# The recurrence's output gate moved from GpSimd (tokens on partitions) to VectorE (features on partitions)

## The reference, cut to what matters

```python
proj = jnp.einsum('bsd,de->bse', rms_norm(x, attn_norm_g), w_in)
qd, kd, vd, qr, fr, ir, gr = jnp.split(proj, SPLIT_POINTS, axis=-1)
od = differential attention of qd, kd, vd, normalised by head
orr = hgrn2_chunked(silu(qr), 1 - f, ir, log f)        # gated linear recurrence
orr = rms_norm(orr, hgrn_norm_g) * jax.nn.silu(gr)      # the gate of this case
mix = jnp.concatenate([od, orr], axis=-1)
x = x + mix @ w_out;  x = x + SwiGLU(rms_norm(x))
```

## Time and profile before

| what | value |
|---|---|
| median of three runs | 2685.63 us (2679.19 to 2687.0) |
| profiled execution | 2681.91 us, span 2680.2 us |
| TensorE busy | 2565.4 us, 96% |
| VectorE busy | 1574.3 us, 59% |
| ScalarE busy | 1143.0 us, 43% |
| GpSimd busy | 900.8 us, 34% |
| granted TensorE clock, mean | 0.985 |

### The profile page before, as it was taken

The page is one execution under the profiler, slowest core; times in us unless marked ns, Lnnn a source line. Parts: engine busy times, 40 slices in busy tenths (PEclk is TensorE's granted clock), DMA queues, the critical chain, the costliest instruction groups (busy, mean ns, idle before and its releaser), DMA issues. The chain is left out here.

```text
span 2680.2 us, 39239 instructions
## 1 busy us (share of the span) xinstructions
PE 2565.4 (96%) x15720; PEld 2150.4 (80%) x15720; DVE 1574.3 (59%) x1927; ACT 1143.0 (43%) x1917; POOL 900.8 (34%) x601
## 2 busy tenths in 40 slices
PE   7999999999898989888999999999999999999999
PEld 6888888887787878786877888887888887888887
DVE  5424344332777777776567666667666666456653
ACT  4434334332467777775563222224232223322221
POOL 4001100000515151404446554554555452236300
PEclk9999999999899999998999999999999999999999
DMA  4755565474544444317784333336334335777763
GB/s 158 266 173 191 196 209 186 137 255 131 136 103 116 107 116 107 86 53 241 235 292 144 103 112 92 106 103 196 106 104 116 93 100 186 260 263 276 240 202 130
DMA packets 343909, 430.79 MB, mean 161 GB/s; under 512 B 19248, under 2 KB 212784, under 8 KB 341040
## 3 DMA queue, kind: packets, MB, share of 16 engines
q1 hardware_dynamic: 343728, 428.29, 50.7%
HBM read 301.87 MB, written 129.50 MB: 161 GB/s over the span
## 5 line engine op out<-in xcount | busy, mean ns | idle before, releaser
L629 DVE TENSOR_TENSOR proj_w_lo<-proj_w_raw,proj_w_hi 128x2048 fp32r<-128x2048 f32 x56 | 130.1, 2323 | 230.1 <-ACT proj_w_hi L529 230.1
L791 PE MATMUL proj_prod<-proj_w_hi,proj_h_lo 128*128 128x512 f32 x640 | 250.1, 391 | 0.0
L1897 ACT ACTIVATE feed_a_hi<-lend_shared 128x1024 fp32r<-128x1024 f32 (+1 forms) x78 | 93.8, 1202 | 286.7 <-PE feed_v_bank L2201 142.0
L1195 ACT ACTIVATE att_expo<-att_ring,att_neg_max 128x1024 f32<-128x1024 f32 (+4 forms) x192 | 164.9, 862 | 101.8 <-DVE att_neg_max L1316 65.7
L2199 PE MATMUL feed_y_bank<-feed_b_hi,feed_a_hi 128*128 128x512 f32 x416 | 165.7, 398 | 16.4 <-DVE feed_results L2054 10.3
L1897 ACT ACTIVATE feed_a_hi<-ahead_full 128x1024 fp32r<-128x1024 f32 (+1 forms) x78 | 93.4, 1202 | 186.1 <-PE feed_y_bank L2201 136.9
L2018 DVE TENSOR_TENSOR feed_a_lo<-lend_shared,feed_a_hi 128x1024 fp32r<-128x1024 f32 (+1 forms) x78 | 148.5, 1904 | 26.8 <-ACT feed_a_hi L1897 26.8
L2201 PE MATMUL feed_y_bank<-feed_b_hi,feed_a_lo 128*128 128x512 f32 x416 | 163.8, 394 | 0.0
L2199 PE MATMUL feed_v_bank<-feed_b_hi,feed_a_hi 128*128 128x512 f32 x416 | 162.9, 392 | 0.4 <-DVE feed_results L2072 0.4
L2201 PE MATMUL feed_v_bank<-feed_b_hi,feed_a_lo 128*128 128x512 f32 x416 | 162.0, 389 | 0.0
L2200 PE MATMUL feed_v_bank<-feed_b_lo,feed_a_hi 128*128 128x512 f32 x416 | 161.9, 389 | 0.0
(11 more groups left out here) (337 smaller groups left out, 7335.4 us busy)
## 6 DMA issues: line engine op xcount, KB each, us to landing
proj_w_raw<-in_w_in_dram SPq DMA_DIRECT2D x56, 1024.0 KB, 6.5
lend_shared<-in_w_gate_dram SPq DMA_DIRECT2D x88, 256.0 KB, 4.0
ahead_full<-in_w_up_dram SPq DMA_DIRECT2D x88, 256.0 KB, 4.0
ff<-ahead_results SPq DMA_DIRECT2D x88, 256.0 KB, 2.5
ff<-ahead_ff_sum SPq DMA_DIRECT2D x66, 256.0 KB, 3.2
operands<-ahead_results SPq DMA_DIRECT2D x48, 256.0 KB, 3.2
lend_lent<-ff SPq DMA_DIRECT2D x28, 384.0 KB, 3.3
down_f_raw<-ff SPq DMA_DIRECT2D x28, 384.0 KB, 3.3
```

Of the source, the lines that this page charges most:

```text
L629: nc.vector.tensor_tensor(w_lo[n % 2][:], w_raw[n % 2][:], w_hi[n % 2][:].bitcast(F32), ALU.subtract).then_inc(w_lo_made, 1)
L791: last = pe.matmul(prod[t][:], lo[:, s, tile], wh[:, k, :], start=False, stop=stop)
L1195: nc.scalar.activation(expo[b][:, m, key:key + width], ring[:, bank * 512:bank * 512 + width], ACT.Exp, bias=neg_max[:, b, m:m + 1], accum ...
L1897: nc.scalar.activation(a_hi[:, first:end], full[g % 2][:, first:end], ACT.Copy).then_inc(a_hi_made, 1)
```

## The change

The gate stays in feature form from the projection on. `project` computes the group HG with the weights stationary, as HQ and HF, and `hgate` has the shape (W, SEQ). In `mix_tokens` the GpSimd product L1154 and the semaphore `r_gated` are gone. Chunks 4 to 7 are no longer copied by ScalarE: VectorE reads the transposed chunk from PSUM, multiplies by the column of gains and by the gate's rows, and writes the stage buffer, one step after the chunk was transposed, ahead of `maximum(s, 0)`. It signals `chunk_gated`, which takes the place of `slot_taken` and of `staged` for these chunks. SyncE loads the gate of block h once the four chunks of head h - 1 are gated (from step 11 of head h on) and ahead of the next block's k, instead of at step 6. The order of head 3's chunks becomes 0, 4, 5, 1, 6, 2, 7, 3, and their taking is shared between the engines.

```diff
-                    HI: lambda: [tokens("hv")], HG: lambda: [tokens("hgate")]}[kind(gi)]()
+                    HI: lambda: [tokens("hv")], HG: lambda: [features("hgate")]}[kind(gi)]()
-                        if kind(gi) in (HQ, HF):
+                        if kind(gi) in (HQ, HF, HG):
-    LAST_CHUNKS = (0, *range(TURNS, CHUNKS), *range(1, TURNS))
+    LAST_CHUNKS = (0, TURNS, *(c for n in range(1, TURNS) for c in (TURNS + n, n)))
+    GATED, TAKEN = [key[0] == "f" and key[2] >= TURNS for key in SLOT], []
+    for n, gates in enumerate(GATED):
+        TAKEN.append(GATED[:n + 1].count(gates))
+        rgate = r.sb("gate", [P, HEADS, TB])
+        def wait_taken(eng, slot):
+            eng.wait_ge(chunk_gated if GATED[slot] else slot_taken, TAKEN[slot])
             def store(h, c):
-                sp.wait_ge(staged, n + 1)
+                if c < TURNS:
+                    sp.wait_ge(staged, h * TURNS + c + 1)
+                else:
+                    sp.wait_ge(chunk_gated, h * HEADS + c - TURNS + 1)
-                    sp.wait_ge(r_gated, h)
-                    load_tokens(rgate, "hgate", h, rgate_in)
+                sp.wait_ge(chunk_gated, h * HEADS)
+                load_features(sp, mid["hgate"], h, rgate[:], rgate_in)
-                nc.gpsimd.tensor_tensor(ro[:], ro[:], rgate[:], ALU.mult).then_inc(r_gated, 1)
-                    act.wait_ge(r_gated, h + 1)
+                    act.wait_ge(fill_read, filled(h, len(FILLS) - 1))
                 for head, c in chunks_at(s):
-                    take_chunk(head, c)
+                    if c < TURNS:
+                        take_chunk(head, c)
+            def gate_chunk(h, c):
+                slot, n = SLOT["f", h, c], chunk_number(h, c)
+                dve.wait_ge(slot_turned, slot + 1)
+                dve.wait_ge(rgate_in, 16 * (h + 1))
+                if h == HEADS - 1:
+                    dve.wait_ge(slot_turned, SLOT["w", TOTAL - 2, groups_of(TOTAL - 2) - 1] + 1)
+                elif n >= STAGES:
+                    dve.wait_ge(stored[n % STAGES], 16 * (n // STAGES))
+                nc.vector.scalar_tensor_tensor(out=staged_at(h, c), in0=turned[slot % 2][:], scalar=rg_col[:],
+                                               in1=rgate[:, c - TURNS, :], op0=ALU.mult, op1=ALU.mult).then_inc(chunk_gated, 1)
                 if early:
                     combine(s - 1)
+                for head, c in chunks_at(s - 1) if s < TOTAL else ():
+                    if c >= TURNS:
+                        gate_chunk(head, c)
                 if live:
                     maximum(s, 0)
...
                     nc.vector.tensor_tensor(first_b[0], first_b[0].bitcast(F32), first_hi.bitcast(F32), ALU.subtract)
+                    gate_chunk(HEADS - 1, TURNS)
                 if s == TOTAL + 1:
+                    gate_chunk(HEADS - 1, TURNS + 1)
                     invert_last_roots()
                     normalise_late(LATE_CHUNKS[-1])
+                    for c in range(TURNS + 2, CHUNKS):
+                        gate_chunk(HEADS - 1, c)
```

More of the change, by code:

```diff
@@ L957, in mix_tokens @@
         rq, rk, rf = early.rows(0), early.rows(1), early.rf
-        rv, rgate = (r.sb(n, [P, CH, W]) for n in ("v", "gate"))
+        rv = r.sb("v", [P, CH, W])
+        rgate = r.sb("gate", [P, HEADS, TB])
         whole = [None] + [r.sb(f"whole{m}", [P, HEADS * TB >> m]) for m in range(1, LEVELS + 1)]
@@ L1008, in mix_tokens @@
         r_summed = r.sem("summed")
-        r_gated = r.sem("gated")
+        chunk_gated = r.sem("chunk_gated")
         r_rms_made = r.sem("rms_made")
@@ L1101, in _ @@
                     load_tokens(rv, "hv", 0, rv_in)
-                    load_tokens(rgate, "hgate", 0, rgate_in)
                 if not last:
@@ L1147, in behind_combination @@
                     pool.wait_ge(combined, step)
-            def gate(h):
-                pool.wait_ge(rgate_in, 16 * (h + 1))
-                pool.wait_ge(fill_read, filled(h, len(FILLS) - 1))
-                if h + 1 < HEADS:
-                    pool.wait_ge(combined, (h + 1) * STEPS - 1)
-                nc.gpsimd.tensor_tensor(ro[:], ro[:], rgate[:], ALU.mult).then_inc(r_gated, 1)
             nc.gpsimd.memset(rscore[:], 0.0).then_inc(scores_cleared, 1)
@@ L1187, in _ @@
                     product(h + 1, LEVELS - 1)
-                gate(h)
         @block.scalar
@@ L1212, in take_chunk @@
                     act.wait_ge(stored[n % STAGES], 16 * (n // STAGES))
-                col = g_col if c < TURNS else rg_col
-                nc.scalar.activation(staged_at(h, c), turned[slot % 2][:], ACT.Copy, scale=col[:]).then_inc(slot_taken, 1)
-                act.wait_ge(slot_taken, slot + 1)
+                nc.scalar.activation(staged_at(h, c), turned[slot % 2][:], ACT.Copy, scale=g_col[:]).then_inc(slot_taken, 1)
+                wait_taken(act, slot)
                 act.sem_inc(staged, 1)
@@ L1388, in normalise_late @@
                     dve.wait_ge(r_rrms_made, HEADS)
-                    dve.wait_ge(r_gated, HEADS)
+                    dve.wait_ge(fill_read, filled(h, len(FILLS) - 1))
                     head = c - TURNS
@@ L1470, in open_slot @@
                 if slot >= 2:
-                    pe.wait_ge(slot_taken, slot - 1)
+                    wait_taken(pe, slot - 2)
             def turn(s, g):
@@ L1484, in weigh @@
                 h, j = divmod(s, STEPS)
-                pe.wait_ge(slot_taken, SLOT["w", s, g] + 1)
+                wait_taken(pe, SLOT["w", s, g])
                 if g == 0 and s:
@@ L2515, in hybrid_trunk_kernel @@
         "hq": scratch("hq", (W, SEQ)), "hf": scratch("hf", (W, SEQ)), "hk": scratch("hk", (W, SEQ)),
-        "hv": scratch("hv", (SEQ, W)), "hgate": scratch("hgate", (SEQ, W)),
+        "hv": scratch("hv", (SEQ, W)), "hgate": scratch("hgate", (W, SEQ)),
     }
```

## The result

| kernel | median of 12 runs | lowest to highest | profiled execution | its span | mean granted clock |
|---|---|---|---|---|---|
| before | 2685.59 us | 2679.19 to 2693.46 | 2681.91 us | 2680.2 us | 0.985 |
| after | 2696.59 us | 2691.18 to 2702.38 | 2697.78 us | 2696.1 us | 0.980 |

The ratio after to before is 1.0041, with an interval from 1.0030 to 1.0051. The forecast was 2685 us with a range up to 2694; the change costs 11 us, and the sum had it at +1.3. Most of what the change does came as the working had it. One term (the product of step 8, +2.3 us) was too small by a factor of three, and another (the end of the stage, -1.0 us) had the wrong sign.

What follows compares the result with a forecast made beforehand. TensorE, busy 96%, was taken as the bound, its gaps in `mix_tokens` hanging on a chain headed by VectorE. Terms 0 + 0 + 0 + 0 + 2.3 - 1.0 = +1.3 us gave 2683.2 or 2686.9; forecast 2685 us, range 2676 to 2694.

Steps and rivals of the forecast that it cites:

- The product of step 8: `mix_tokens`, three heads: VectorE's new product delays maximum, exponentials and TensorE's next score by its length, +2.3 us.
- the end of the stage: End of `mix_tokens`: last chunk taken 1.9 us sooner, so last `mix` stores and `feed` come sooner, -1.0 us.
- Projection: `project`: four gate groups move to feature form with matmul number and size unchanged, cost 0.
- GpSimd's product: `mix_tokens`: four GpSimd products of 4.54 us go, none on the path, worth 0.
- ScalarE's copies: `mix_tokens`, heads 1 to 3: twelve copies go, 10.1 us of ScalarE's time, taken as worth 0.
- The rival that ScalarE was the limit: `mix_tokens`: the saved 0.84 us in twelve places reach TensorE, -8.8 us in all, 2675 us; chance 0.12.
- The products of steps 9 to 11: `mix_tokens`, nine places: products of 0.75 us fit VectorE's gaps of about 0.96 us ahead of the maxima, cost 0.
- the slower rival: `mix_tokens`: GpSimd's reads hold up the new products or they don't fit, +10.2 us, 2694 us; chance 0.14.
- The rule that was weighed there: VectorE with two SBUF inputs blocks against GpSimd reading SBUF; with at most one, like the new product, it doesn't.
- The upper bound of 6.7 us: Step 8's product in three heads: cost of 3 x (0.75 + 1.49) us if GpSimd holds it up.
- The waits added: `mix_tokens`: VectorE's wait for a stored stage buffer and the later gate load, 0 for both.
- ScalarE's wait for the stores: `feed`: sign that the forecast is right, ScalarE's wait for `mix` falls from 2.39 us to below 1 us.

Runs made afterwards that it cites:

- e5_no_pool: Kernel before, with GpSimd's product of the gate done on one column instead of all: 2686.53 us, ratio 0.9996.
- e2_behind_max: Changed kernel with VectorE's product in step 8 put behind the first maximum instead of ahead of it: 2688.66 us, ratio 1.0002.
- e14_behind_old_order: Changed kernel with step 8's product behind the first maximum and the last head's chunks in the order of the kernel before: 2688.33 us, ratio 1.0006.
- e11_one_step_later: Changed kernel with the chunks of heads 0 to 2 turned one step later (FIRST_CHUNK_STEP 4 in place of 3): 2689.85 us, ratio 1.0009.
- e12_later_old_order: Changed kernel with FIRST_CHUNK_STEP 4 in place of 3 and the last head's chunks in the old order: 2686.68 us, ratio 1.0004.
- e7_extra_gaps: Kernel before, with an added VectorE reduction of 512 columns in steps 9, 10 and 11 of heads 1 to 3: 2685.04 us, ratio 0.9999.
- e3_one_column: Changed kernel with its twelve VectorE products of heads 0 to 2 working on one column of 512: 2689.87 us, ratio 1.0008.
- e8_combine_behind: Changed kernel with step 8's product and also its joining put behind the first maximum: 2689.10 us, ratio 1.0007.
- e1_repeat: The changed kernel again, unchanged, for a second profile: 2693.42 us, ratio 1.0027.
- e4_extra_512: Kernel before, with an added VectorE reduction of 512 columns between joining and first maximum in step 8 of heads 1 to 3: 2695.08 us, ratio 1.0029.
- e9_old_order: Changed kernel with the last head's chunks in the order of the kernel before: 2694.33 us, ratio 1.0031.
- 256 columns: Kernel before, with an added VectorE reduction of 256 columns between joining and first maximum in step 8 of heads 1 to 3: 2691.92 us, ratio 1.0018.
- e15_before_again: The kernel before, unchanged, profiled and timed as if it were another: 2686.34 us, ratio 1.0003.

## Why the prediction was wrong

**Projection, 0: right.** The sigmoid's tiles take 0.60 us with 2.12 us of idle time ahead, as in the earlier trace rows.

**GpSimd's product, 0: right,** as e5_no_pool shows to within its interval.

**ScalarE's copies, 0: right.** The rival that ScalarE was the limit, which had 10.1 us for the copies, falls: in the four versions without them and without the step-8 delay (e2_behind_max, e14_behind_old_order, e11_one_step_later and e12_later_old_order) the lower ends of the intervals are 0.9991 to 0.9998, at most 2.4 us of gain.

**The products of steps 9 to 11, 0: right.** e7_extra_gaps shows the cover in the kernel before. In the changed one head 3 has no fall there, and its distances are 13.11 - 12.45 = 0.66 us for the product of step 8, and 8.04 us as before: nothing for the others. The price of 0.75 us was right too; the sixteen products from the lines (min/median/max ns) are

```profile
L1405 DVE SCALAR_TENSOR_TENSOR att_stage<-att_turned,early_rg_col,rec_gate x12: 750/751/752, 848.1 to 1145.4; 128x512 f32<-128x512 f32 x12
L1405 DVE SCALAR_TENSOR_TENSOR att_expo<-att_turned,early_rg_col,rec_gate x4: 746/751/752, 1208.7 to 1215.6; 128x512 f32<-128x512 f32 x4
```

and the one at 876.40 ran beside a row of GpSimd products that read SBUF, without being held:

```profile
874.72 2.92 POOL L1151 TENSOR_TENSOR rec_whole<-rec_whole 128x512 f32<-128x512 f32 x5
876.40 0.75 DVE L1405 SCALAR_TENSOR_TENSOR att_stage<-att_turned,early_rg_col,rec_gate 128x512 f32<-128x512 f32 x1 [1.53 <-PE att_turned L1524]
```

So the slower rival, whose 2694 us lies near the measured time, came near it by luck: its mechanism isn't there. The rule that was weighed there (the Trainium skill, "SBUF — State Buffer", "Who interferes with whom") agrees with this trace: two of the sixteen products, at 876.40 and 1010.25, lie wholly beside such GpSimd products, and with the column scalar and the one tensor in SBUF they take 0.75 us like the others.

**The product of step 8, +2.3 us: this is the step that failed.** The delay itself came nearly as worked out: 3 x 0.66 = 2.0 us for 2.3, TensorE's wait 1.87 us for 1.9 to 2.0. What it left out is what TensorE does after a wait. I read TensorE's wait and never the PEclk of the windows behind it, and took the cost of a delay to be the delay. The distance from step 6's joining to step 9's, summed over heads 1 to 3, has a mean of 83.5 us in the eleven profiles without the delay, e3_one_column and e8_combine_behind among them (81.7 to 84.7), and of 90.5 us in the four with 0.66 to 0.7 us of it (after, e1_repeat, e4_extra_512 and e9_old_order, 88.2 to 92.9). That is 7.0 us, not 2.3: 2.0 us of delay and 5.0 us of lower clock, in step 8 (1.5 us in 9 of 12 places) and step 9 (1.6 us in 9 of 12 places, against 13 of 33 without). The part in step 9, about 1.7 of the 5.0 us, rests on few places and is the less certain: with 256 columns none of three heads fell there. The upper bound of 6.7 us comes near by luck too, since it stood there for a hold-up by GpSimd that isn't there.

**The waits added, 0: right** but for the two waits on a bank that VectorE holds, 1.1 us in all at the stage's end.

**The end of the stage, -1.0 us: wrong in sign.** I had the last chunk 1.9 us sooner; it is 1.0 us. And `feed` doesn't wait for the chunk but for its store, which lands later than before: the split starts 22.9 us after the last joining, and 22.4 in the kernel before, +0.5 us, of which the new order is +1.0. (The eight profiles of the kernel before and of its variants have 21.7 to 22.8 us, with a mean of 22.2, the six with the new order a mean of 23.1: +0.9 us.) ScalarE's wait for the stores, which was to be below 1 us, is 2.41 us. The barrier is still set by VectorE's two sums, as said.

**The sum.** 7.0 + 0.5 = 7.5 us, or 7.9 with +0.9 us for the end. The two measurements of the change have ratios of 1.0041 and 1.0027, 11.0 and 7.3 us. What lies between is within the intervals (0.1% is 2.7 us each way), and so is not explained. One thing more is open: from TensorE's first use of `feed_y_bank` to the end, where the change has nothing, the profile has 2696.1 - 1227.5 = 1468.6 us, and e15_before_again 1463.8; the profiles with 0.66 us of delay or more have 1467.5 to 1470.8 there, those without it 1463.8 to 1470.0, so the ranges overlap. Why they differ isn't found. As to the chances: the medians of the kernel before in the five sessions lie within 1.7 us (2685.6 to 2687.3), where the prediction allowed 8 us between two medians of one kernel.

## What to carry to other kernels

When an edit makes the engine that bounds the kernel wait longer, count the delay and then look at the granted clock behind that wait: here each 0.66 us of it drew 1.7 us more on average. Put new work on the feeding engine behind the instruction that the bounding engine waits for; one place in the order was worth 7 to 10 us (1.0002 against 1.0027 and 1.0041), where the work saved on ScalarE and GpSimd was worth none that shows. And a stage's end that waits for stores need not be sooner because their sources are: read when they land.

## What the runs showed of the hardware

- Whether the clock falls behind one and the same wait differs between the heads and between executions of one program: with 1.87 to 1.93 us of standing in step 8 it fell in two heads and not in the third, and in the repeat, with 1.93 us in each, in all three. The fall itself costs nearly the same each time: 1.5 to 1.6 us in either step.
- Back to back, the product of 0.75 us holds the next VectorE instruction up by 0.66 us; the joining of 1.29 us ahead of it held the product up by 1.32 us.
- Eight stores of 256 KB took 4.9 us (median) to land in one order of issue and 3.9 us in another; the last seven were issued within 4.94 and 5.88 us.
